# ScalarE takes over copies, the first convolution tap and the high parts in the first block

## The chip, the cores and the metric

The program runs on one core of a Trainium2 chip. The metric is the device time of one launch in microseconds (us). A core has TensorE (PE in the profile, its weight loads are PEld), VectorE (DVE), ScalarE (ACT), GpSimd (POOL) and SyncE (SP), which only issues transfers here. Each engine works through its own instructions in order, and they meet through semaphores.

## What is computed

Two transformer blocks stand behind each other. The change touches only the first mixer of the first one: a differential attention over 256 tokens with four heads, beside it a convolution and a gated linear recurrence in both directions, then one output projection over both.

```python
def even_mixer(h, ...):                      # shortened
    q, k, v, g, xr, gr = split(h @ w_in)     # 24 blocks of 128 channels, tokens along the free axis
    a = diff_attention(q, k, v, t5_table, lam, lam_init, subln_g)
    r = bidir_rglru(xr, conv_w, conv_b, w_a, b_a, w_x, b_x, lru_lambda)
    return concat(a * silu(g), r * silu(gr)) @ w_out

def diff_attention(q, k, v, ...):
    p = softmax(q @ k.T * scale + bias)      # two maps for each head
    out = (p[0] - lam * p[1]) @ v
    return rms_norm(out, subln_g) * (1.0 - lam_init)

def bidir_rglru(x, ...):
    xc = conv(x, conv_w, padding=(2, 1)) + conv_b        # four taps, per channel
    gate_a, gate_x = sigmoid(xc @ w_a + b_a), sigmoid(xc @ w_x + b_x)
    log_a = -8.0 * gate_a * softplus(-lam)
    u = sqrt(-expm1(2.0 * log_a)) * gate_x * xc
    return scan_forward(exp(log_a), u) + scan_backward(exp(log_a), u)
```

## The kernel before

Activations lie transposed: 128 channels on the partitions, tokens along the free axis. `ev` holds the 24 projected blocks, `xc` the four convolved ones, `OT` the four attention outputs, `gates`, `aT` and `tT` what the recurrence needs. Every matrix product is made to full precision out of three matmuls: a value x is split into a high part `Hh` (rounded to the fp32r type) and a low part `Hl` = x - Hh, and so is each weight tile (`Wh` by ScalarE at L526, `Wl` by VectorE at L811). `three` issues the three matmuls of one 128x128 block. The weight tiles come through `raw`, two slots of 1 MB.

The order of each engine is written out by hand and doesn't change at run time. A helper `link` makes VectorE wait for its own last instruction. The order around the change is this.

- **Convolution.** After the last tile of even_in, and after small work for lambda, VectorE makes for each of the four blocks one tensor_scalar (tap 2 and the bias, L1115) and three linked multiply-adds (L1116 to L1118, recorded at L798, as all its `scalar_tensor_tensor` are). Each block releases matmuls with the gate weights `lruw`; 16 products in all, whose tanh ScalarE makes into `gates` (L672). Meanwhile ScalarE has made the exponential for lambda (L658), copied the T5 row table and sent it out and in again by DMA (L662, L665), and copied the turned values `evtok` (L668).
- **Attention.** Four groups g of two query blocks make eight units u. TensorE: scores (u + 2), `mix` of the group before (in even units from 2 on), transposes of u. VectorE: `maxes` of u + 1, `normalise` of u, and in even units from 2 on `take` (L999), which waits for the mix and copies it from the PSUM tile `psN` to `OT`. ScalarE: `exps` of u + 1 (L610), two activations of the recurrence (`decay`, L677 and L678), `copies` of u (L625). The fourth mix and its take stand behind the loop.
- **Subnorm.** ScalarE squares `OT` (L681), makes the tanh of the gate, splits a weight tile and takes the square root that the recurrence needs (L687). TensorE sums the squares over channels, 16 matmul records on `psN`. VectorE multiplies the gates (two of 1024 columns, three of 2048, up to L1132), then computes the means (L1134). GpSimd raises them to -0.5, TensorE spreads the result.
- **Output projection.** VectorE scales `OT`, multiplies it by the gate (L1143), makes high and low part of each of its four blocks (L992, L993), then does the product with the square root, eight scans, a sum, and, after a tanh by ScalarE (L690), the last two products (L1157, L1158) and the parts of the other four blocks. `h_ready` counts the blocks with both parts. TensorE multiplies the first two tiles of even_out with blocks 0 to 3 (48 matmuls) when they come, and with 4 to 7 when these come.
- **SyncE.** In even_out it sends for each tile t: the weight tile t + 2, two gemv weights (`ada_w` or `mod_w`), each after a dot product of VectorE has freed a slot (L840), and from t = 1 on four loads of the neighbourhood bias `nab` (L411), the first after `h_ready` of all eight blocks.

## Time and profile before

| | |
|---|---|
| time, median of 3 runs | 2087.09 us (2086.03 to 2087.93) |
| profiled execution | 2086.57 us, span 2084.8 us |
| granted TensorE clock, mean | 0.961 |
| TensorE busy | 1910.5 us, 92% |
| VectorE busy | 1403.1 us, 67% |
| ScalarE busy | 683.8 us, 33% |
| GpSimd busy | 123.0 us, 6% |

The times of rows are microseconds from the start of the span. The profiled execution's time is 1.8 us longer than its span. Busy shares are means over stages with different limits. The stretch that the change touches lies between about 120 and 207 us, and what it releases reaches to about 250 us.

### The profile page before, as it was taken

The page shows a single profiled execution, that of the slowest core. Times are in us where ns is not written, and L with a number is a line of the kernel's source. Part 1 is how long each engine was busy: PE and PEld are TensorE (multiplying, and loading weights), DVE is VectorE, ACT ScalarE, POOL GpSimd, SP SyncE. Part 2 cuts the span into 40 slices and gives each one's busy share as a digit, 9 for nine tenths or more (in the row PEclk, how much of TensorE's full clock was granted, in tenths as well). Part 3 has the DMA queues.
Part 4 walks back from the last instruction along what each step waited for, and adds up shares of the span by engine and source line. Part 5 has one row for each costly group of instructions (what it writes and reads, how often), then busy time and mean ns, then how long its engine had stood idle before and what let it go on. Part 6 is the DMA issues. An engine that isn't in the chain of part 4 may idle for free.

```text
span 2084.8 us, 26715 instructions
## 1 busy us (share of the span) xinstructions
PE 1910.5 (92%) x10092; PEld 1624.6 (78%) x10092; DVE 1403.1 (67%) x2091; ACT 683.8 (33%) x910; POOL 123.0 (6%) x78
## 2 busy tenths in 40 slices
PE   2975799799999998997999999989999998889998
PEld 2954788678888887886888888878888887679998
DVE  7868899876666666668766666776665225856554
ACT  2443356332222223332322222132222123444432
POOL 2000200200000110002000001100000010010000
PEclk9976899899999999998999999999999999999999
DMA  9840955433334443434244334424433323223444
GB/s 377 309 176 26 247 193 198 156 120 141 133 148 148 154 172 121 151 131 159 113 151 149 133 140 168 167 110 151 151 138 115 101 93 120 91 81 141 164 162 158
DMA packets 75738, 315.79 MB, mean 151 GB/s; under 512 B 19060, under 2 KB 22904, under 8 KB 56344
## 3 DMA queue, kind: packets, MB, share of 16 engines
q1 hardware_dynamic: 75136, 314.15, 42.6%
q8 instruction: 37, 0.61, 0.1%
q10 hardware_dynamic: 536, 0.79, 0.1%
q14 instruction: 29, 0.24, 0.0%
HBM read 313.86 MB, written 1.06 MB: 151 GB/s over the span
## 4 chain that ended last, share of the span: by engine, by line
PE 74%; DVE 17%; ACT 3%; issue 2%; DMA 1%; SPq 1%; POOL 0%; DVEq 0%; ACTq 0%
PE acc L1296 72%; DVE Wl L811 4%; ACT Wh L526 2%; DVE tmp L798 2%; PE psN L1296 1%; DVE psGT L843 1%; DVE psGT L846 1%; DVE najunk L846 1%; DVE najunk L843 1%; DMA afirst<-in_ada_w 1%; DVE small L968 1%; DVE XT L798 1%; DVE psGT L840 1%; DVE tmp L986 1%; PE psN L1358 0%
## 5 line engine op out<-in xcount | busy, mean ns | idle before, releaser
L1296 PE MATMUL acc<-Hh,Wh 128*128 128x512 f32 (+1 forms) x2320 | 808.4, 348 | 50.1 <-DVE Hl L798 24.2
L1296 PE MATMUL acc<-Hl,Wh 128*128 128x512 f32 (+1 forms) x2320 | 800.3, 345 | 0.0
L1296 PE MATMUL acc<-Hh,Wl 128*128 128x512 f32 (+1 forms) x2320 | 799.6, 345 | 0.0
L811 DVE TENSOR_TENSOR Wl<-raw,Wh 128x2048 fp32r<-128x2048 f32 (+1 forms) x214 | 449.6, 2101 | 273.4 <-ACT Wh L526 273.3
L1296 PEld LDWEIGHTS acc<-Hh,Wh 128*128 128x128 f32 x2320 | 448.3, 193 | 113.7 <-issue 46.0
L526 ACT ACTIVATE Wh<-raw 128x2048 fp32r<-128x2048 f32 (+1 forms) x214 | 374.3, 1749 | 350.0 <-PE acc L1296 331.8
L1296 PEld LDWEIGHTS acc<-Hl,Wh 128*128 128x128 f32 x2320 | 448.6, 193 | 50.7 <-issue 0.7
L1296 PEld LDWEIGHTS acc<-Hh,Wl 128*128 128x128 f32 x2320 | 447.9, 193 | 50.4
L1296 PE MATMUL acc<-hidh,Wh 128*128 128x512 f32 (+1 forms) x704 | 258.6, 367 | 0.9 <-DVE Wl L811 0.9
L1296 PE MATMUL acc<-hidl,Wh 128*128 128x512 f32 (+1 forms) x704 | 258.3, 367 | 0.0
L1296 PE MATMUL acc<-hidh,Wl 128*128 128x512 f32 (+1 forms) x704 | 258.2, 367 | 0.0
L798 DVE SCALAR_TENSOR_TENSOR tmp<-tmp,acc 128x512 f32<-128x512 f32 (+1 forms) x176 | 109.4, 621 | 129.7 <-ACT tmp L593 120.0
L593 ACT ACTIVATE tmp<-acc 128x512 f32<-128x512 f32 (+1 forms) x88 | 47.9, 544 | 452.8 <-PE acc L1296 452.8
L843 DVE SCALAR_TENSOR_TENSOR psGT<-graw,cb 128x1024 f32<-128x1024 f32 x122 | 169.3, 1388 | 0.4
L459 POOL TENSOR_TENSOR tmp<-tmp 128x512 f32<-128x512 f32 (+1 forms) x44 | 90.1, 2049 | 1310.6 <-ACT tmp L557 1152.5
L846 DVE SCALAR_TENSOR_TENSOR psGT<-graw,cb 128x1024 f32<-128x1024 f32 x122 | 154.0, 1262 | 4.2
L1296 PEld LDWEIGHTS acc<-hidh,Wh 128*128 128x128 f32 x704 | 132.4, 188 | 25.1 <-DVE Wl L811 1.1
L1296 PEld LDWEIGHTS acc<-hidh,Wl 128*128 128x128 f32 x704 | 132.3, 188 | 23.9
L1296 PEld LDWEIGHTS acc<-hidl,Wh 128*128 128x128 f32 x704 | 132.4, 188 | 23.8
L935 DVE TENSOR_TENSOR hidl<-tmp,hidh 128x512 f32 (+3 forms) x88 | 55.1, 626 | 71.5 <-ACT hidh L596 71.5
L798 DVE SCALAR_TENSOR_TENSOR XT<-acc,mod,XT 128x256 f32 (+3 forms) x88 | 36.0, 455 | 88.5 <-PE acc L1296 88.5
L596 ACT ACTIVATE hidh<-tmp 128x512 f32 (+3 forms) x88 | 50.9, 578 | 134.1 <-DVE tmp L798 134.1
(222 smaller groups left out, 1189.9 us busy)
## 6 DMA issues: line engine op xcount, KB each, us to landing
raw<-in_ffn_up SPq DMA_DIRECT2D x88, 1024.0 KB, 4.8
graw<-in_mod_w SPq DMA_DIRECT2D x144, 512.0 KB, 5.5
raw<-in_ffn_down SPq DMA_DIRECT2D x64, 704.0 KB, 4.1
graw<-in_ada_w SPq DMA_DIRECT2D x32, 512.0 KB, 6.8
raw<-in_odd_in SPq DMA_DIRECT2D x16, 1024.0 KB, 5.0
raw<-in_even_in SPq DMA_DIRECT2D x12, 1024.0 KB, 7.2
raw<-in_conv_in SPq DMA_DIRECT2D x12, 1024.0 KB, 4.8
afirst<-in_ada_w SPq DMA_DIRECT2D x8, 1024.0 KB, 13.1
```

Of the source, the lines that this page charges most:

```text
L459: nc.gpsimd.tensor_tensor(tmp[:, 2, 0:n], tmp[:, 0 if k == 1 else 2, 0:n], tmp[:, k % 2, 0:n], ALU.add).then_inc(n_sum, 1)
L526: nc.scalar.activation(Wh[:, half, 0:f], raw[:, slot, 0:f], ACT.Copy).then_inc(hi_ready, 1)
L593: nc.scalar.activation(tmp[:, b, 0:s.tokens], acc[b][0][:, 0:s.tokens], ACT.Tanh, scale=0.5)\
L596: nc.scalar.activation(at3(hidh, t, s.tokens), tmp[:, 3, 0:s.tokens], ACT.Copy).then_inc(ffn_hi, 1)
L798: return nc.vector.scalar_tensor_tensor(out=out, in0=a, scalar=s, in1=b, op0=op0, op1=op1)
L811: nc.vector.tensor_tensor(Wl[:, half, 0:f], raw[:, slot, 0:f], Wh[:, half, 0:f].bitcast(f32), ALU.subtract)\
L840: nc.vector.scalar_tensor_tensor(out=psGT[:, :], in0=graw[:, slot, :], scalar=0.5, in1=cfirst[:, :], op0=ALU.mult, op1=ALU.mult, accum_out ...
L843: nc.vector.scalar_tensor_tensor(out=junk[:, :], in0=graw[:, slot, :], scalar=0.5, in1=cb[:, 0, :], op0=ALU.mult, op1=ALU.mult, accum_out= ...
L846: nc.vector.scalar_tensor_tensor(out=junk[:, :], in0=graw[:, slot, :], scalar=0.5, in1=cb[:, 1, :], op0=ALU.mult, op1=ALU.mult, accum_out= ...
L935: nc.vector.tensor_tensor(at3(hidl, t, c), tmp[:, 3, c], at3(hidh, t, c).bitcast(f32), ALU.subtract)\
L968: link(nc.vector.tensor_reduce(out=out, in_=L[:, u % 2, :, :], op=ALU.max, axis=AX.X))
L1296: return nc.tensor.matmul(out, lhsT, rhs, start=start, stop=stop)
```

## The change

In the first mixer some work passes from VectorE to ScalarE, and some work is cut or reordered.

- ScalarE writes tap 2 and the bias of all four convolution blocks, in one go behind the last projection copy and ahead of the exponential for lambda.
- ScalarE copies the four mixed outputs from `psN` to `OT` (`output`), in the loop behind `copies(u)`, the last one behind the loop. VectorE has no take in this attention any more.
- The high parts `Hh` of the eight blocks are written by ScalarE (`parts`): four behind the square root, four behind the tanh at L690. VectorE writes the low parts alone (`low_part`).
- The product of `OT` with its gate, one instruction of 1024 columns, becomes four of 256, each with a semaphore for ScalarE; the last product of the recurrence likewise.
- The low parts of blocks 0 to 3 come after the product with the square root, where both parts came before it.

```diff
+        lru_tap, ev_full, ev_hi = sem("lru_tap"), sem("ev_full"), sem("ev_hi")
...
+            def output(g):
+                act.wait_ge(diff.mixed, g + 1)
+                nc.scalar.activation(OT[:, g, :], psN[:, 0:LAT], ACT.Copy).then_inc(diff.taken, 1)
+
             def attention(a, beside=None):
                 exps(a, 0)
                 for u in range(a.units):
...
                     copies(a, u)
+                    if a is diff and u >= 2 and u % 2 == 0:
+                        output(u // 2 - 1)
+                if a is diff:
+                    output(a.groups - 1)
...
             project(S["even_in"], lambda m: at(ev, m), beside_even_in)
 
+            act.wait_ge(drained["act"], S["even_in"].drained1)
+            for c in range(4):
+                nc.scalar.activation(xc[:, c, :], ev[:, 16 + c, :], ACT.Identity, scale=V("conv_w", c * 4 + 2), bias=V("conv_b", c))\
+                    .then_inc(lru_tap, 1)
             act.wait_ge(lam_sum, 1)
...
             nc.scalar.activation(tT[:, :, :], tT[:, :, :], ACT.Sqrt).then_inc(lru_mult, 1)
+            def parts(c, x):
+                act.wait_ge(ev_full, c + 1)
+                nc.scalar.activation(Hh[:, c, 0:LAT], x, ACT.Copy).then_inc(ev_hi, 1)
+
+            for c in range(4):
+                parts(c, OT[:, c, :])
             act.wait_ge(lru_hs, 1)
 
             nc.scalar.activation(aT[:, 0:4, :], ev[:, 20:24, :], ACT.Tanh, scale=0.5).then_inc(ev_th, 1)
+            for c in range(4):
+                parts(4 + c, gates[:, 1, c, :])
...
-            def two_parts(k, value, width=LAT):
-
-                link(nc.vector.tensor_copy(Hh[:, k, 0:width], value))
-                nc.vector.tensor_tensor(Hl[:, k, 0:width], value, Hh[:, k, 0:width].bitcast(f32), ALU.subtract).then_inc(h_ready, 1)
+            def low_part(k, value):
+
+                dve.wait_ge(ev_hi, k + 1)
+                nc.vector.tensor_tensor(Hl[:, k, 0:LAT], value, Hh[:, k, 0:LAT].bitcast(f32), ALU.subtract).then_inc(h_ready, 1)
...
-                if a is diff:
-                    nc.vector.tensor_copy(OT[:, g, :], o).then_inc(a.taken, 1)
-                elif a is na:
+                if a is na:
...
-                    if u >= 2 and u % 2 == 0:
+                    if a is gqa and u >= 2 and u % 2 == 0:
                         take(a, u // 2 - 1)
-                take(a, a.groups - 1)
+                if a is gqa:
+                    take(a, a.groups - 1)
...
-                link(nc.vector.tensor_scalar(y, x, V("conv_w", c * 4 + 2), V("conv_b", c), ALU.mult, ALU.add))
+                dve.wait_ge(lru_tap, c + 1)
...
-            link(stt(OT[:, :, :], OT[:, :, :], 0.5, sga, ALU.mult, ALU.mult))
             for c in range(4):
-                two_parts(c, OT[:, c, :])
+                stt(OT[:, c, :], OT[:, c, :], 0.5, sga[:, c, :], ALU.mult, ALU.mult).then_inc(ev_full, 1)
             dve.wait_ge(lru_mult, 1)
             u_ = gates[:, 1, :, :]
             link(stt(u_, u_, 0.5, tT[:, :, :], ALU.mult, ALU.mult))
+            for c in range(4):
+                low_part(c, OT[:, c, :])
...
-            link(stt(gates[:, 1, 0:4, :], gates[:, 1, 0:4, :], 0.5, aT[:, 0:4, :], ALU.mult, ALU.mult))
             for c in range(4):
-                two_parts(4 + c, gates[:, 1, c, :])
+                stt(gates[:, 1, c, :], gates[:, 1, c, :], 0.5, aT[:, c, :], ALU.mult, ALU.mult).then_inc(ev_full, 1)
+            for c in range(4):
+                low_part(4 + c, gates[:, 1, c, :])
```

## Rows read from the trace of the kernel before

**Rows 1.** The page's chain that ended last, shares of the span by engine.

```profile
PE 74%; DVE 17%; ACT 3%; issue 2%; DMA 1%; SPq 1%; POOL 0%; DVEq 0%; ACTq 0%
```

**Rows 2.** Windows: stretch, length, busy time of each engine (instructions), clock, DMA share, GB/s.

```profile
core 0: us, PE busy (x) PEld busy (x) DVE busy (x) ACT busy (x) POOL busy (x), PEclk, DMA share, GB/s
142.02:171.63 29.61, 19.30 (x64) 9.93 (x64) 22.45 (x67) 19.07 (x56) 0.00 (x0) 0.67 0.00 0
...
188.85:206.57 17.72, 10.88 (x63) 10.68 (x64) 16.20 (x28) 1.06 (x1) 1.00 (x2) 0.70 0.00 1
206.57:235.86 29.29, 20.70 (x152) 20.00 (x151) 24.23 (x29) 10.05 (x12) 13.59 (x8) 0.91 1.13 240
```

**Rows 3.** Timeline, convolution: start, duration, engine, line, tiles, count, idle before and releaser.

```profile
123.89 0.20 ACT L658 ACTIVATE small<-small 128x2 f32<-128x2 f32 x1 [2.24 <-DVE small L1107]
...
124.70 0.41 DVE L1115 TENSOR_SCALAR xc<-ev_proj,vec 128x256 f32<-128x256 f32 x1
125.15 1.52 DVE L798 SCALAR_TENSOR_TENSOR xc<-ev_proj,vec,xc 128x254 f32<-128x254 f32 x3
126.59 0.40 DVE L1115 TENSOR_SCALAR xc<-ev_proj,vec 128x256 f32<-128x256 f32 x1
...
132.37 8.73 PE L1296 MATMUL acc<-xc,lruw 128*128 128x256 f32 x26 [0.66 <-DVE xc L798]
```

**Rows 4.** Groups by line and form, 124 to 206 us: count, busy us, mean ns.

```profile
L678 ACT ACTIVATE tT<-gates,small 128x256 f32<-128x256 f32 x8 | 4.7, 586 | 0.0
...
L993 DVE TENSOR_TENSOR Hl<-OT,Hh 128x256 fp32r<-128x256 f32 x4 | 1.7, 426 | 0.1
...
L992 DVE CAST Hh<-OT 128x256 fp32r<-128x256 f32 x4 | 1.2, 288 | 0.0
```

**Rows 5.** Timeline of the attention, VectorE and what it waits for.

```profile
154.08 0.42 DVE L999 COPY OT<-psN 128x256 f32<-128x256 f32 x1 [1.13 <-PE psN L1296]
...
154.43 0.74 DVE L798 SCALAR_TENSOR_TENSOR tmp<-acc,t5b 128x256 f32<-128x256 f32 x2
...
157.23 0.75 DVE L798 SCALAR_TENSOR_TENSOR tmp<-acc,t5b 128x256 f32<-128x256 f32 x2
...
160.54 0.42 DVE L999 COPY OT<-psN 128x256 f32<-128x256 f32 x1 [0.42 <-PE psN L1296]
...
167.39 0.37 ACT L625 ACTIVATE dP<-psGT 128x256 f32<-128x256 f32 x1
...
169.52 2.07 PE L1296 MATMUL psN<-dP,evtok 128*128 128x256 f32 x4 [0.47 <-ACT dP L625]
...
171.63 0.42 DVE L999 COPY OT<-psN 128x256 f32<-128x256 f32 x1 [3.33 <-PE psN L1296]
```

**Rows 6.** Timeline behind the attention, to the product of OT and gate.

```profile
171.97 2.47 DVE L798 SCALAR_TENSOR_TENSOR gates<-gates,xc 128x1024 f32<-128x1024 f32 x2
...
173.20 3.58 PE L1296 MATMUL psN<-ones,tmp 128*128 128x1 f32 x16 [1.61 <-ACT tmp L681]
...
180.28 0.16 DVE L1134 TENSOR_SCALAR means<-psN 128x8 f32<-128x8 f32 x1
...
186.70 1.22 DVE L798 SCALAR_TENSOR_TENSOR OT<-OT,tmp 128x1024 f32<-128x1024 f32 x1
```

**Rows 7.** Timeline of the output projection: ScalarE's tanh and the first dot product.

```profile
199.00 1.06 ACT L690 ACTIVATE aT<-ev_proj 128x1024 f32<-128x1024 f32 x1 [15.39 <-DVE gates L1155]
...
205.26 1.23 DVE L840 SCALAR_TENSOR_TENSOR psGT<-graw,cfirst 128x1024 f32<-128x1024 f32 x1
```

**Rows 8.** The chain in order of time: even_in's matmuls, even_out's with its fifth block.

```profile
99.99 15.22 PE acc L1296 x124
...
203.41 4.47 PE acc L1296 x24
```

**Rows 9.** Timeline of SyncE's queue, and the ScalarE split that waits for it.

```profile
218.07 9.40 SPq L411 DMA_DIRECT2D nab<-in_na_rpb  x4
227.52 1.45 SPq L373 DMA_DIRECT2D raw<-in_odd_in  x1
...
235.86 1.91 ACT L526 ACTIVATE Wh<-raw 128x2048 fp32r<-128x2048 f32 x1 [2.16 <-DMA raw<-in_odd_in]
```

## The prediction

> **What bounds the kernel now.** I read the page's chain first. It puts 74% of the span on TensorE and 17% on VectorE [rows 1], so a VectorE edit can pay only in a stretch in which TensorE waits. The windows show two such stretches in the first block: during the attention TensorE is busy for 19.30 of 29.61 us, and during the output projection the DMA engines are over full (share 1.13) [rows 2]. I then went through the timeline of each engine from 120 to 236 us, asking at each step what ended the wait. The reader is to see five stages, each started by the one before: the convolution on VectorE, which releases the gate matmuls [rows 3]; the attention, where VectorE's step and its copy of the mixed output alternate [rows 5]; a VectorE chain that ends in the means of the subnorm [rows 6]; the two halves of even_out, each released by a low part [rows 7, 8]; and a SyncE queue and transfers set off by VectorE's first dot product [rows 7, 9]. SyncE has nothing with a date of its own between 121 and 206 us: what it sends is released by VectorE or TensorE, and the DMA share is 0.00 from 188.85 to 206.57 [rows 2]. So time saved up to 206 us should stay saved.
>
> **Stage 1, the convolution.** Removed from VectorE: four tensor_scalars. A channel starts every 1.89 us (124.70 to 126.59), of which the tap with its link takes 0.45 (124.70 to 125.15) [rows 3]. A channel then takes 1.44, and the matmuls that the fourth releases at 132.37 start 4 x 0.45 sooner, at 130.57. **Gain 1.8.** TensorE has 26 matmul instructions in 8.73 us there without a break, so the gain passes through to the first score. ScalarE's new taps have per-partition scale and bias, as the decay at L678 has: 586 ns [rows 4], about 0.49 from one start to the next with the overlap, so 2.1 us in all. The next ScalarE work, the exponential of lambda, starts at 123.89 after 2.24 us of idleness [rows 3], so the last projection copy ends at 121.65, and the taps run from there to about 123.75. The cover is thus nearly used up: every tenth of a microsecond that the taps take beyond 2.2 delays that exponential, and with it the T5 transfers behind it and the whole VectorE chain. If the cover were gone the price would be all of 2.1, more than the gain; I charge nothing, and keep 0.3 for the range.
>
> **Stage 2, the attention.** Between takes, a VectorE step is 2.80 (154.43 to 157.23) [rows 5]. In a step with a take it also waits for the mix and copies: 1.13 + 0.42 the first time [rows 5], 0.42 + 0.42 the second [rows 5], and the third is a copy alone, less the 0.08 by which neighbours overlap: 1.5, 0.85 and 0.34. If VectorE stays last, the eighth normalise comes 2.7 earlier. ScalarE takes the copies over, at the length of its like copy dP from PSUM, 0.37 [rows 5]. They stand behind copies(u), which waits for a transpose that TensorE issues after the mix, so that output(g) finds its semaphore set; queued behind it are the exponentials of the next step. ScalarE is busy for 19.07 us in the eight steps [rows 2], 2.4 a step, and with the outputs 2.6, under 2.80. But around each mix the order copies, output, exponentials lies on the way to the next normalise, and there ScalarE gives back its 0.37 twice. At the end, copies(6) and mix(3) stand 2.13 apart now (167.39 to 169.52); then copy, output, two decays of 0.49 and copy fill 2.1 there, so this distance stays. **Gain 1.9**, with bounds 0 (ScalarE holds the old pace) and 2.7.
>
> **Stage 3, from the last mix to the means.** The last mix ends at 169.52 + 2.07 = 171.59. VectorE sat idle for it for 3.33 us, copied, and only then began the gate work that leads at 180.28 to the means [rows 5, 6]: 8.69 after the mix. That work (171.97 to 180.28, 8.31 long) needs nothing of the mix. Without the take it starts when the last normalise ends: 3.33 before the mix's copy, plus the 0.8 by which stage 2 brings VectorE further forward than the mix, so about 4.1 before the mix ends, and it is through 8.3 - 4.1 = 4.2 after it. Then another is late: the copy, the square and the 16 sums end at 173.20 + 3.58 = 176.78 [rows 6], 5.2 after the mix, and the copy is no longer on ScalarE than on VectorE. **Gain 8.69 - 5.2 = 3.5.** The square root on ScalarE comes after its split and a table load; its wait is for the same gate work, and its result is wanted only after the OT products, so it is covered by some 5 us. If stage 2 gains nothing, this stage still holds, because the TensorE sums set it.
>
> A rule of the Trainium skill bears on ScalarE's order here ("ScalarE: Activation LUTs", section "Table sets: the hidden batching unit"): copy and identity are in every table set, so the high parts right after the square root should load nothing. No run here shows a copy after a square root. By the rule nothing is added; if it failed, one more load would fall into ScalarE's idle time before the Tanh, and the sum would be the same.
>
> **Stage 4, OT to the second half of even_out.** One product of 1024 columns, 1.22 (186.70) [rows 6], becomes four of 256: a three-operand instruction of this size takes 0.48 and starts 0.40 after its neighbour where no link stands between (the three of a channel end at 125.15 + 1.52 = 126.67, the next starts at 126.59) [rows 3], so 4 x 0.40 instead of 1.24: +0.36. Casts go: a pair of cast and difference is 0.66, four pairs 2.65 (0.288 and 0.426 with their links) [rows 4]; four differences alone, 0.35 apart, are 1.4. Before the scans that is 2.65 - 1.4 - 0.36 = 0.9 saved. The gates product of 2048 columns now stands ahead of the low parts, and VectorE's high parts come from ScalarE, which has been idle for 15.39 us at its next instruction [rows 7] and has them ready meanwhile. The order delays the first half of even_out: with 7.2 gained up to here, the product of 186.70 starts at 179.5, the four parts of it end at 181.1, the gates product (2048 columns, as long as two of 1024 less one fixed part, 2.3) at 183.4, the first low part at 183.8. TensorE then needs 8.9 for 48 instructions at the pace of 24 in 4.47 [rows 8], until 192.7. The second half is released at 203.41 - 8.1 = 195.3, so the delay is covered by 2.6. Behind the Tanh, four products at 0.40 and a difference (2.03) stand for product, cast and difference (1.22 + 0.29 + 0.43), which cost 0.1 more with the split: nothing. **Gain 0.9.** The fourth difference, and with it the first dot (205.26) [rows 7], comes some 0.9 sooner still: the three pairs behind the first, 3 x 0.66, become 3 x 0.35.
>
> The fixed cost of small pieces is the rule that speaks against this change ("VectorE: DVE Perf Modes", section on the TRN2 errata: an SBUF-source instruction pays a fixed latency each, tiles of 512 or more amortise it). The trace agrees: 1024 columns take 1.22 and 256 take 0.48. By the page's formula (N+151)/0.96 a split would cost 4 x 0.424 - 1.224 = 0.47, an estimate; the total would be 0.1 less for each split.
>
> **Stage 5, SyncE and the transfers.** The two ada_w loads wait for the dots, and the bias loads stand behind them. Four bias loads take 9.40 us to issue, the second odd_in tile goes out at 227.52 and is used at 235.86 [rows 9], with the DMA engines full [rows 2]. So this stretch starts with the first dot, 8.1 + 0.9 = 9.0 earlier, but the dots of the second tile follow TensorE, 8.1 earlier, and SyncE waits for them once more. Result between 8.1 and 9.0; I take 8.8, as a full DMA queue bridges that wait.
>
> **The sum.** 1.8 + 1.9 + 3.5 + 0.9 = 8.1, and 0.7 of the 0.9: 8.8. The profiled execution took 2086.57 with a span of 2084.8; its span becomes 2076.0, its time 2077.8, and against the median of 2087.09, 0.5 above it, **2078.3**.
>
> **The rivals.** (a) ScalarE's order holds the attention at its old pace: 8.8 - 1.9 = 6.9, 2080.2. For it: ScalarE is busy for 19.07 of 29.61 us there and gets work inside a loop of waits. Against: 2.6 of work in 2.80. (b) The clock gives more: the granted clock is 0.67 in the attention [rows 2], so the engine changes between 1.2 and 2.4 GHz there; after its pause it runs even_out's second half at 24 instructions in 4.47 us, where 124 of even_in took 15.22 [rows 8], 2.95 for 24. With the pause cut to under 4 us it might start at the high level: up to 1.5 more, 10.3, 2076.8. (c) The gain is absorbed: the transfers of stage 5 stay where they are because the queue, not its start, sets their landing. For it: share 1.13, a landing of 8.3 us. Against: the DMA engines stand still before 206 us, so the stretch can start early. If the landing at 235.86 moved by half of the 9.0 only, less 0.5 for the wait on the second tile's dots, 4.0 would be left: 2083.1. (d) Slower, by the clock alone: granted clock falls in the stage after the change. A tile of odd_in has 48 instructions, 5.9 at the pace of even_in; at half the clock it costs up to 5.9 more. From two such tiles it eats the gain, and three make 17.7: 2096.0. For it: that stage begins after a pause and at the low level already. Against: nothing in the change makes later pauses longer. (e) The work moves to ScalarE without any wait of VectorE going: 1.8 + 0.9 + 0.9 alone, 3.6, which is less than can be told, 2083.5. Against it stands the idle time of 3.33 in rows 5.
>
> **How the numbers follow.** Forecast 0.55; (a) 0.17; (b) 0.15; (c) 0.05; (d) 0.03; (e) 0.05. Measurement tells 0.2%, 4.2 us, from no change. The forecast's own range is 8.1 to 9.6, less 0.3 for the taps: 2077.5 to 2079.3. With (a), its lower bound for stage 5 (6.2) and (b) with stage 2 at its upper bound (11.1), and up to 0.5 of scatter, the range is 2075.5 to 2081.5. Faster by over 0.2%: 0.55 + 0.17 + 0.15 = 0.87; within: 0.10; slower: 0.03.
>
> **What would show it.** The last convolution instruction near 130.5; ScalarE's taps over before 123.9; VectorE without idle time before an OT copy and the last mix ending near 167.9; the means near 173.1, released by the sums and no longer by VectorE; the first matmul of even_out near 183.8 and the fifth input block's near 195.3; the second odd_in tile used near 227. I am wrong if ScalarE's taps push the T5 chain, if exponentials start later in the loop, if the table is loaded more than three times on the path, or if odd_in's first matmul isn't some 8.8 earlier.

## The result and the profile after

The changed kernel takes a median of 2076.84 us (2075.76 to 2079.23, 5 runs) against 2087.49 for the kernel before on the same chip: the ratio is 0.9948, with a 95% interval from 0.9938 to 0.9959. By the ratio 10.9 us are gone, where 8.8 were forecast. The time lies inside the whole range, and is faster than the forecast's own range of 2077.5 to 2079.3. The profiled execution took 2075.76 with a span of 2073.9.

The page's part 4 of the changed kernel, the chain's shares:

```profile
PE 74%; DVE 18%; ACT 3%; issue 2%; DMA 1%; POOL 1%; SPq 0%; DVEq 0%; ACTq 0%
```

At 10 us in 2000 the shares tell nothing. The windows tell more. These are the attention, the stretch around even_out's two halves, and the stretch of the odd_in weights (share of the DMA engines and GB/s are the last two columns, the granted clock stands before them):

```profile
137.56:164.60 27.04, 16.63 (x64) 8.74 (x64) 24.74 (x67) 19.58 (x60) 0.00 (x0) 0.78 0.00 0
180.39:193.58 13.19, 9.53 (x58) 9.33 (x59) 11.97 (x23) 2.48 (x5) 1.00 (x2) 0.76 0.01 1
193.58:222.36 28.78, 20.60 (x146) 19.91 (x145) 24.23 (x29) 10.14 (x11) 13.30 (x8) 0.86 1.12 247
```

The attention shrank from 29.61 to 27.04 [rows 2]; ScalarE is busy for 19.58 in it, where it was for 19.07. The timeline of the changed kernel, convolution and attention (start, length, engine, line, operation, count, idle time before it and what ended it; TensorE, VectorE and ScalarE rows are picked out):

```profile
119.70 0.66 ACT L543 ACTIVATE ev_proj<-acc 128x256 f32<-128x256 f32 x2 [3.30 <-PE acc L1318]
120.39 2.07 ACT L668 ACTIVATE xc<-ev_proj,vec 128x256 f32<-128x256 f32 x4
122.60 0.20 ACT L671 ACTIVATE small<-small 128x2 f32<-128x2 f32 x1
123.41 5.82 DVE L819 SCALAR_TENSOR_TENSOR xc<-ev_proj,vec,xc 128x254 f32<-128x254 f32 x12
129.28 7.35 PE L1318 MATMUL acc<-xc,lruw 128*128 128x256 f32 x26 [0.21 <-DVE xc L819]
137.56 1.14 PE L1318 MATMUL acc<-ev_proj 64*128 64x256 f32 x8 [0.93 <-ACT gates L685]
...
148.41 0.75 DVE L819 SCALAR_TENSOR_TENSOR tmp<-acc,t5b 128x256 f32<-128x256 f32 x2
...
151.23 0.75 DVE L819 SCALAR_TENSOR_TENSOR tmp<-acc,t5b 128x256 f32<-128x256 f32 x2
...
154.04 0.75 DVE L819 SCALAR_TENSOR_TENSOR tmp<-acc,t5b 128x256 f32<-128x256 f32 x2
...
160.93 2.48 DVE L819 SCALAR_TENSOR_TENSOR gates<-gates,xc 128x1024 f32<-128x1024 f32 x2
162.49 2.07 PE L1318 MATMUL psN<-dP,evtok 128*128 128x256 f32 x4 [0.73 <-ACT dP L626]
164.60 0.38 ACT L631 ACTIVATE OT<-psN 128x256 f32<-128x256 f32 x1 [2.17 <-PE psN L1318]
166.12 3.58 PE L1318 MATMUL psN<-ones,tmp 128*128 128x1 f32 x16 [1.56 <-ACT tmp L694]
169.73 0.17 DVE L1154 TENSOR_SCALAR means<-psN 128x8 f32<-128x8 f32 x1 [0.41 <-PE psN L1318]
```

The reader is to see four things. The twelve convolution instructions stand in one row of 5.82, without the tap. ScalarE's taps are one row of 2.07 and the exponential follows them without a noted wait, 2.90 after the last projection copy as in before. VectorE's steps begin 2.82 and 2.81 apart (148.41, 151.23, 154.04) with and without a mix between them, where 154.08, 160.54 and 171.63 were copies with waits [rows 5]. And the gate work begins at 160.93, 3.63 before the last mix ends (162.49 + 2.07), so that the means are released by TensorE's sums and no longer by VectorE [rows 6].

The output projection of the changed kernel, the same view:

```profile
176.16 1.43 DVE L819 SCALAR_TENSOR_TENSOR OT<-OT,tmp 128x256 f32<-128x256 f32 x4
176.61 1.43 ACT L703 ACTIVATE Hh<-OT 128x256 fp32r<-128x256 f32 x4 [4.57 <-DVE OT L819]
177.50 2.28 DVE L819 SCALAR_TENSOR_TENSOR gates<-gates,tT 128x2048 f32<-128x2048 f32 x1
178.06 1.28 ACT L709 ACT_TABLE_LOAD   x1
179.82 1.43 DVE L1014 TENSOR_TENSOR Hl<-OT,Hh 128x256 fp32r<-128x256 f32 x4
180.39 0.55 PE L1318 MATMUL acc<-Hh,Wh 128*128 128x256 f32 x1 [5.84 <-DVE Hl L1014]
191.40 0.58 PE L1318 MATMUL acc<-Hh,Wh 128*128 128x256 f32 x1 [3.66 <-DVE Hl L1014]
192.27 1.23 DVE L861 SCALAR_TENSOR_TENSOR psGT<-graw,cfirst 128x1024 f32<-128x1024 f32 x1
222.36 1.89 ACT L527 ACTIVATE Wh<-raw 128x2048 fp32r<-128x2048 f32 x1
```

Four products of 256 columns take 1.43, and so do the four low parts. The second odd_in tile is used at 222.36 without a wait, where at 235.86 the transfer was waited for [rows 9].

**Where the time went.** I compare by the distances between events, since the last even_in copy came at 120.99 in the profiled execution of before, at 119.70 here, and anywhere from 119.35 to 120.99 in the fourteen traces of this study: nothing changed ahead of it, so that is the execution's scatter. All in us, worked out from the starts in the traces; "before, again" is a second execution of the same kernel, taken with the last group of experiments:

```
                                              forecast gain  before  before, again   after
last even_in copy -> first score                   1.8        21.03      20.70       17.86
first score -> last mix                            1.9        27.50      28.02       24.93
last mix -> means                                  3.5        10.76      10.76        7.24
means -> fifth block's first matmul                0.9        23.13      23.13       21.67
sum                                                8.1        82.42      82.61       71.70
means -> first dot                                 1.8        24.98      24.98       22.54
fifth block -> first tile of even_out complete     -           4.56       5.58        5.58
that tile -> norm means of odd_in                  -          28.88      28.61       28.62
norm means of odd_in -> end of the span            -        1848.0     1849.0      1848.3
last even_in copy -> end of the span               8.8      1963.8     1965.8      1954.2
```

Up to the fifth block 10.7 are gained against the first execution of before, 10.9 against the second. Behind it the changed kernel is like the second execution of before to 0.01 up to the norm means. The first one differs in three places, none of them the change's doing: it is 1.02 faster to the complete tile, 0.26 slower to the norm means, and from there to the first scaled block 3.18 pass, where both others have 4.38 (e5 and e6 take this up). What follows scatters by up to 0.9 more. So by the last row 9.6 are gained against one execution and 11.6 against the other.

### The profile page after: what moved, and what is told of

It is laid out like the page before. It is cut to its first block, busy times and chain, and to the rows that moved or that the text cites. A ratio compares the mean times of both kernels' runs of the same rounds, so it can differ in the third digit from the quotient of the medians.

```text
span 2073.9 us, 26722 instructions
## 1 busy us (share of the span) xinstructions
PE 1906.5 (92%) x10092; PEld 1621.9 (78%) x10092; DVE 1397.0 (67%) x2081; ACT 689.9 (33%) x926; POOL 128.0 (6%) x78
## 4 chain that ended last, share of the span: by engine, by line
PE 74%; DVE 18%; ACT 3%; issue 2%; DMA 1%; POOL 1%; SPq 0%; DVEq 0%; ACTq 0%
PE acc L1318 72%; DVE Wl L832 4%; ACT Wh L527 2%; DVE tmp L819 2%; PE psN L1318 1%; DVE psGT L861 1%; DVE psGT L867 1%; DVE psGT L864 1%; DVE najunk L867 1%; DVE najunk L864 1%; DVE small L989 1%; DVE XT L819 1%; DMA afirst<-in_ada_w 1%; PE psN L1380 1%; DVE tmp L1007 1%
```

## The experiments

Eight kernels change the changed kernel (e), three the kernel before (f2 to f4), and f1 is the kernel before again. Times are medians; the ratio is to the kernel before on the same chip. The e kernels from e1 to e4 were run beside 2088.06 for before, e5 to e8 beside 2087.71, the f kernels beside 2087.77. Two medians of different groups are thus from different chips, and each ratio of e1 to e8 is known only to 0.001 to 0.0017 either way, 2 to 3.5 us. The changed kernel's interval is 0.9938 to 0.9959. Of the e kernels only e3 lies clear of it by its time; for the others the differences of medians are not told from scatter, and the distances in the traces carry the reading.

### e1: the taps back on VectorE

```diff
-            act.wait_ge(drained["act"], S["even_in"].drained1)
-            for c in range(4):
-                nc.scalar.activation(xc[:, c, :], ev[:, 16 + c, :], ACT.Identity, scale=V("conv_w", c * 4 + 2), bias=V("conv_b", c))\
-                    .then_inc(lru_tap, 1)
...
-                dve.wait_ge(lru_tap, c + 1)
+                link(nc.vector.tensor_scalar(y, x, V("conv_w", c * 4 + 2), V("conv_b", c), ALU.mult, ALU.add))
```

> The changed kernel with the first tap of the convolution back on VectorE, all else as changed. Measured from the start of ScalarE's last copy of even_in, the changed kernel releases the fourth channel's gate matmuls after 9.6 us and starts the first score after 17.9 us; the kernel before needed 11.4 and 21.0. Theory: the tap is worth 4 x 0.45 = 1.8 us at the fourth channel (11.4 again) and the other 1.4 us at the first score is the TensorE clock that rises earlier when the gate matmuls stand closer together, so the first score goes back to about 21.0 and the time is 1.8 to 3.2 above the changed kernel. Rival: the 1.4 us is chance of the clock from run to run; then the first score comes 1.8 later only (19.7).

**Measured:** 2079.77, ratio 0.9961 (0.9947 to 0.9975), 2.9 above the changed kernel. Copy to first score is 21.10, so 3.24 come back there and not 1.8; the loop behind it takes 25.08. The 26 gate matmuls take 8.79, where they took 7.35.

### e2: three of the four outputs back on VectorE

```diff
-                    if a is diff and u >= 2 and u % 2 == 0:
-                        output(u // 2 - 1)
...
-                if a is na:
+                if a is diff:
+                    nc.vector.tensor_copy(OT[:, g, :], o).then_inc(a.taken, 1)
+                elif a is na:
...
-                    if a is gqa and u >= 2 and u % 2 == 0:
+                    if u >= 2 and u % 2 == 0:
                         take(a, u // 2 - 1)
```

> The changed kernel with VectorE taking the first three mixed outputs again inside the loop, and ScalarE only the last. Theory: the last mix starts some 2.6 us later relative to the first score (24.9 us in the changed kernel, 27.5 before), and VectorE's gate work behind the loop, being later by 2.7, ends about when the sums of TensorE do; means and all that follows 2.6 to 3 later. Rival: the pace of the loop was set by TensorE's clock (granted 0.78 against 0.67), so the last mix comes less than 1 us later.

**Measured:** 2080.72, ratio 0.9961 (0.9947 to 0.9975), 3.9 above the changed kernel. First score to last mix is 28.47, 3.54 longer; every other distance is the changed kernel's. The three copies of e2 on VectorE in its timeline:

```profile
150.00 0.42 DVE L1018 COPY OT<-psN 128x256 f32<-128x256 f32 x1 [1.11 <-PE psN L1318]
...
156.99 0.42 DVE L1018 COPY OT<-psN 128x256 f32<-128x256 f32 x1 [0.94 <-PE psN L1318]
...
163.55 0.42 DVE L1018 COPY OT<-psN 128x256 f32<-128x256 f32 x1 [0.51 <-PE psN L1318]
```

The waits are 1.11, 0.94 and 0.51, where [rows 5] have 1.13 and 0.42, and the third copy there came without one. A copy behind a wait costs the wait and its full 0.42, so these terms make 3.82. VectorE is that much later: the reciprocal of the last unit, with which its normalise begins, starts 25.94 after the first score, 22.13 in the changed kernel. The last mix is only 3.54 later, since with e2 ScalarE's third output copy is gone as well. It had pushed back by 0.27 the last of ScalarE's copies of the turned weights to `dP`, for which the last mix waits.

### e3: the last output back on VectorE

```diff
-                if a is diff:
-                    output(a.groups - 1)
...
-                if a is gqa:
-                    take(a, a.groups - 1)
+                take(a, a.groups - 1)
```

> The changed kernel with only the last mixed output taken by VectorE again, which then waits for the last mix before its gate work. Theory: the last mix stays where it is, the means come 8.7 us after its end instead of 5.2: 3.5 us, and the time is some 3.5 above the changed kernel. Rival: the gain behind the loop came out of the earlier loop; then the time is less than 1 us above.

**Measured:** 2081.47, ratio 0.9972 (0.9963 to 0.9982), 4.6 above by the medians and 4.6 by the spans (2078.5 and 2073.9). Last mix to means is 10.76, as before the change, which is 3.52 of it, and the loop keeps its 24.93. The rest stands behind the norm means (1849.8 to the end of the span against 1848.3), where e3 changes nothing and the two executions of before differ by 1.1. VectorE's timeline in e3:

```profile
164.17 0.42 DVE L1018 COPY OT<-psN 128x256 f32<-128x256 f32 x1 [3.59 <-PE psN L1317]
164.51 2.47 DVE L817 SCALAR_TENSOR_TENSOR gates<-gates,xc 128x1024 f32<-128x1024 f32 x2
...
172.82 0.16 DVE L1153 TENSOR_SCALAR means<-psN 128x8 f32<-128x8 f32 x1
```

VectorE stands for 3.59 with the gate work queued behind the copy, and is again the last at the means. The place of one instruction of 0.42 is worth 3.52.

### e4: product, casts and differences as before

```diff
-            for c in range(4):
-                parts(c, OT[:, c, :])
...
-            for c in range(4):
-                parts(4 + c, gates[:, 1, c, :])
...
+            link(stt(OT[:, :, :], OT[:, :, :], 0.5, sga, ALU.mult, ALU.mult))
             for c in range(4):
-                stt(OT[:, c, :], OT[:, c, :], 0.5, sga[:, c, :], ALU.mult, ALU.mult).then_inc(ev_full, 1)
+                two_parts(c, OT[:, c, :])
...
-                low_part(c, OT[:, c, :])
...
+            link(stt(gates[:, 1, 0:4, :], gates[:, 1, 0:4, :], 0.5, aT[:, 0:4, :], ALU.mult, ALU.mult))
             for c in range(4):
-                stt(gates[:, 1, c, :], gates[:, 1, c, :], 0.5, aT[:, c, :], ALU.mult, ALU.mult).then_inc(ev_full, 1)
-            for c in range(4):
-                low_part(4 + c, gates[:, 1, c, :])
+                two_parts(4 + c, gates[:, 1, c, :])
```

> The changed kernel with the output projection as before: one product of 1024 columns, high and low part both by VectorE, ahead of the product with the square root. Theory: between the OT product and the fifth block's first matmul 1.5 us come back (16.7 in place of 15.2), the first dot is 2.4 later, but the second half of even_out may run at the higher TensorE clock again for part of its way (24 instructions in 4.5 us instead of 5.5), so the first matmul of odd_in is only 0.5 to 1.5 later, the time 2077.3 to 2078.5. Rival: the clock has nothing to do with it; then the time is 1.5 to 2.4 above the changed kernel.

**Measured:** 2078.93, ratio 0.9962 (0.9948 to 0.9976), 2.1 above the changed kernel. Means to fifth block is 23.13 (1.46 back) and means to first dot 24.98 (2.44 back). The split of the first half in e4's timeline:

```profile
177.34 1.22 DVE L811 SCALAR_TENSOR_TENSOR OT<-OT,tmp 128x1024 f32<-128x1024 f32 x1
178.60 0.29 DVE L1005 CAST Hh<-OT 128x256 fp32r<-128x256 f32 x1
178.93 0.43 DVE L1006 TENSOR_TENSOR Hl<-OT,Hh 128x256 fp32r<-128x256 f32 x1
179.27 0.28 DVE L1005 CAST Hh<-OT 128x256 fp32r<-128x256 f32 x1
...
181.26 2.28 DVE L811 SCALAR_TENSOR_TENSOR gates<-gates,tT 128x2048 f32<-128x2048 f32 x1
```

From the product's start to the gates product 3.92 pass here. In the changed kernel 1.34 pass, and the low parts, which follow later, put 1.35 between the gates product and the first scan (179.82 to 181.17): 1.23 less in all up to the scans. The other 0.24 is behind the Tanh, where from the product's start to the fifth block 2.06 pass in before (201.35 to 203.41) and 1.82 in the changed kernel (189.58 to 191.40).

### e5 and e6: the split of an odd_in tile out of the norm's chain

By the trace of the changed kernel the stretch behind the first half ends in this chain (VectorE, then GpSimd, in the timeline of the changed kernel):

```profile
225.60 0.16 DVE L897 TENSOR_SCALAR means<-psN 128x4 f32<-128x4 f32 x1 [4.33 <-PE psN L1380]
225.68 2.28 DVE L832 TENSOR_TENSOR Wl<-raw,Wh 128x2048 fp32r<-128x2048 f32 x1
225.84 2.68 POOL L452 TENSOR_TENSOR rctx<-means,expo 128x2 f32<-128x2 f32 x1 [6.70 <-DVE means L897]
```

GpSimd's power on two columns takes 2.68 while VectorE's split reads two arrays in SBUF; in the trace of before the same power took 0.71, and the split began 0.79 after the end of the means instead of at once. e5 moves the split ahead of the wait for the sums, e6 behind the loop that scales the blocks.

```diff
 # e5
+                if name == "odd_in":
+                    split(S[name].n0 + 1, early=True)
                 dve.wait_ge(n_ss, i + 1)
...
-                split(S[name].n0 + 1, early=True)
+                if name != "odd_in":
+                    split(S[name].n0 + 1, early=True)
 # e6
-                split(S[name].n0 + 1, early=True)
+                if name != "odd_in":
+                    split(S[name].n0 + 1, early=True)
...
                     ins.then_inc(h_ready, 1)
+                if name == "odd_in":
+                    split(S[name].n0 + 1, early=True)
```

> The changed kernel with VectorE's split of odd_in's second weight tile moved ahead of its wait for the sums (in the norm ahead of odd_in only). In the changed kernel GpSimd's first power takes 2.68 us beside that split, against 0.71 in the kernel before, where the tile came late and the split started after the powers. Theory: the two engines slow each other; with the split out of the way the power takes 0.7 again, the split fills VectorE's wait of 4.3 us, the means come about 1 us later and the first scaled block some 1.2 us earlier. Rival: the power is long for another reason (code of that instruction cold, a busy memory); then it stays at 2.7 and the scaled block comes 1 us later.

> The changed kernel with the same split moved behind the norm's eight blocks. Theory: the power takes 0.7, the first scaled block comes 2.0 us earlier, and odd_in's first tile ends 2.0 earlier; but the second tile's split is then done some 2.3 us after the norm, later than TensorE wants it, and VectorE's masks and dots are pushed behind it, so 1 us or more is given back on the second tile. Rival (the power is long for another reason): 2.7 stays, and nothing comes earlier.

**Measured:** e5 2076.06, ratio 0.9947 (0.993 to 0.9964); e6 2076.96, ratio 0.9949 (0.9933 to 0.9966). Neither can be told from the changed kernel. The timeline of e5:

```profile
225.41 2.29 DVE L832 TENSOR_TENSOR Wl<-raw,Wh 128x2048 fp32r<-128x2048 f32 x1 [3.80 <-ACT Wh L527]
227.62 0.15 DVE L899 TENSOR_SCALAR means<-psN 128x4 f32<-128x4 f32 x1
227.85 0.71 POOL L452 TENSOR_TENSOR rctx<-means,expo 128x2 f32<-128x2 f32 x1 [8.37 <-DVE means L899]
```

and of e6:

```profile
225.97 0.71 POOL L452 TENSOR_TENSOR rctx<-means,expo 128x2 f32<-128x2 f32 x1 [6.70 <-DVE means L897]
...
235.73 2.29 DVE L832 TENSOR_TENSOR Wl<-raw,Wh 128x2048 fp32r<-128x2048 f32 x1
237.94 1.95 DVE L1195 TENSOR_TENSOR nab<-nab,namask 128x768 f32<-128x768 f32 x2
```

The power takes 0.71 in both, so the split beside it was what stretched it. In e5 the split had to wait 3.80 for ScalarE's high part of the tile, and the means, behind the split, come 1.68 later; the first scaled block follows them after 2.39 instead of 4.38, 1.99 sooner. In e6 the first scaled block stands 2.40 behind the means. Of these 2 us nothing is left later on: from the norm means to the first square of the next norm pass 149.64 in the changed kernel (4.38 + 9.04 + 136.22) and 150.01 in e6 (2.40 + 9.25 + 138.36). VectorE's queue has hardly a gap from here on, and the split that e6 puts behind the blocks lies in it at 235.73, ahead of the mask products, which therefore start at 237.94 where the changed kernel had them at 237.58. That this queue is where the 2 us go is argued from these rows; no run shows it.

### e7: the low parts before the product with the square root

```diff
             for c in range(4):
                 stt(OT[:, c, :], ...).then_inc(ev_full, 1)
+            for c in range(4):
+                low_part(c, OT[:, c, :])
             dve.wait_ge(lru_mult, 1)
...
-            for c in range(4):
-                low_part(c, OT[:, c, :])
```

> The changed kernel with the low parts of blocks 0 to 3 ahead of the product with the square root, as the parts stood before. Theory: the first half of even_out starts 2.2 us earlier, but the second half is released by the same VectorE chain, so the fifth block, first dot and time stay within 0.3 us of the changed kernel, apart from a wait of some tenths for ScalarE's high part. Rival: the shorter pause of TensorE in the changed kernel matters for its clock, and the longer one (5.9 us in place of 3.7) makes the second half slower.

**Measured:** 2076.39, ratio 0.9947 (0.9931 to 0.9964), equal to the changed kernel. TensorE in e7's timeline:

```profile
178.01 0.55 PE L1318 MATMUL acc<-Hh,Wh 128*128 128x256 f32 x1 [3.52 <-DVE Hl L1014]
...
191.33 0.58 PE L1318 MATMUL acc<-Hh,Wh 128*128 128x256 f32 x1 [4.97 <-DVE Hl L1014]
```

The first half starts 13.32 ahead of the second instead of 11.01, and the pause before the second becomes 4.97 instead of 3.66; means to fifth block stays at 21.66. The delay that the change puts on the first half costs nothing. The second half is as slow as in the changed kernel, 5.58 to its completion.

### e8: two more copies at each of three outputs

```diff
             def output(g):
                 act.wait_ge(diff.mixed, g + 1)
+                if g < 3:
+                    nc.scalar.activation(Hh[:, 2 * g + 0, LAT:TOK], psN[:, 0:LAT], ACT.Copy)
+                    nc.scalar.activation(Hh[:, 2 * g + 1, LAT:TOK], psN[:, 0:LAT], ACT.Copy)
                 nc.scalar.activation(OT[:, g, :], psN[:, 0:LAT], ACT.Copy).then_inc(diff.taken, 1)
```

The extra copies go to a part of `Hh` that nothing reads then.

> The changed kernel with two more copies of the mixed output by ScalarE (into an unused part of Hh) ahead of each of the first three copies: 3 x 2 x 0.3 us more work for ScalarE inside the attention loop. Theory (ScalarE has slack at 2.6 of 2.8 us a step, but lies on the way around each mix): most of the 1.8 us shows at the last mix, because copies, output and exponentials follow one another: 1.0 to 1.8 later. Rival: VectorE sets the loop and ScalarE's extra work is hidden: below 0.6 later.

**Measured:** 2078.80, ratio 0.9957 (0.994 to 0.9973), 2.0 above the changed kernel. First score to last mix is 26.86, 1.93 longer, where six copies, each 0.27 after its neighbour, are 1.6. VectorE hardly feels them: its steps stay at 2.81 or 2.82 but for one of 3.03, and its gate work begins only 0.64 later after the first score. What has grown is the chain of ScalarE and TensorE around the mixes: from the dP copy of unit 2 to that of unit 4, and on to that of unit 6, 6.01 and 6.02 pass (150.45, 156.46, 162.48), where two steps of VectorE are 5.62. So two more copies at a mix are not covered. How much of the 1.93 is theirs stays open, since the second and the third mix take 2.08 each here and 1.13 in the changed kernel, at a lower clock.

### f1 to f4: the kernel before again, and with one part of the change each

f1 is the kernel before unchanged (one run, so no ratio). f2 has ScalarE's taps alone, f3 the four outputs alone, f4 the split product with ScalarE's high parts and the new order alone; the edits are those parts of the diff above.

> The kernel before once more, for a second trace of it: what of the differences is chance. In its first trace the gate matmuls took 8.73 us, the second half's first 24 matmuls 4.56, GpSimd's first power 0.71, and the second odd_in tile came late. Theory: the waits of VectorE's chain are the same to 0.1 us (first score to last mix 27.5, mix to means 10.8, means to fifth block 23.1); what TensorE's clock and the DMA engines set may differ by up to 1 us, the power by 2.

> The kernel before with only the first tap moved to ScalarE. Theory: the fourth channel's matmuls are released 9.6 us after the last projection copy instead of 11.4, TensorE's clock rises earlier within them, and the first score comes 3.2 us earlier (17.9), the time 2.5 to 3.4 below the kernel before. Rival (clock by chance): 1.8 earlier.

> The kernel before with only the four output copies moved to ScalarE. Theory: first score to last mix 24.9 instead of 27.5, mix to means 7.2 instead of 10.8, so the means 6.1 earlier relative to the first score, and the time 5 to 6.5 below the kernel before. Rival: the loop's gain needs the other edits' clock; then the loop gives under 1.5 and the total 4 to 5.

> The kernel before with only the output projection changed (products in four pieces, high parts by ScalarE, low parts later). Theory: means to fifth block 21.7 instead of 23.1, the first dot 2.4 earlier, but what follows is timed by the fifth block and VectorE, so the time is 1 to 1.7 below the kernel before, not 2.4. Rival: the earlier dot and its transfers count in full; then 2.4 or more.

**Measured,** with the four distances of each:

```
                    median   ratio (95%)               copy->score  score->mix  mix->means  means->fifth
f1 before, again    2088.07  (one run)                    20.70       28.02       10.76       23.13
f2 taps alone       2085.17  0.9987 (0.9978 to 0.9997)    18.11       28.54       10.76       23.13
f3 outputs alone    2081.85  0.9971 (0.9961 to 0.9982)    20.69       25.08        7.24       23.14
f4 parts alone      2085.89  0.9990 (0.9981 to 1.0)       20.64       28.04       10.76       21.66
changed             2076.84  0.9948 (0.9938 to 0.9959)    17.86       24.93        7.24       21.67
```

Each part moves its own distance and leaves the others but for up to half a microsecond. By the ratios the parts make 0.0013 + 0.0029 + 0.0010 = 0.0052, as much as 1 - 0.9948, but each is known only to about 0.001, and that of f4 isn't told from nothing. By the medians 2.6 come from the taps, 5.9 from the outputs, 1.9 from the parts. The distances are sharper: added up to the fifth block's first matmul, f2 is 2.07 below f1, f3 6.46 and f4 1.51, together 10.04, and the changed kernel is 10.91 below. The taps alone gain 2.59 at the first score and give 0.52 back in the loop, because the second mixed output is waited for longer there (1.00 in f2, 0.51 in f1); without takes in the loop nothing is given back. The rows of the gate matmuls, in f1 and in f2:

```profile
131.83 8.40 PE L1296 MATMUL acc<-xc,lruw 128*128 128x256 f32 x26 [0.66 <-DVE xc L798]
```

```profile
130.05 7.60 PE L1301 MATMUL acc<-xc,lruw 128*128 128x256 f32 x26 [0.21 <-DVE xc L803]
```

The same 26 instructions take 8.40 without the taps moved and 7.60 with them, and between two channels TensorE stands for 0.66 without and 0.21 with them; they take 7.27 to 7.92 in the nine traces where the taps are on ScalarE, and 8.34 to 8.79 in the five where they are not.

## Why the prediction was right in direction and short by two microseconds

**Stage 1 (1.8 forecast, 2.6 to 3.2 measured).** The release of the matmuls moved as worked out: from the last projection copy to the end of the fourth channel pass 11.38 in before and 9.58 in the changed kernel, 1.80 less. The step that failed is "so the gain passes through to the first score": it took the 26 matmuls as 8.73 either way. They run at a granted clock of 0.67 in before, 0.69 in f1, 0.77 in f2 and 0.79 in the changed kernel, so partly at 1.2 and partly at 2.4 GHz, and ahead of them TensorE now stands for 0.21 between two channels instead of 0.66. That is worth another 0.8 (f1 against f2) to 1.4. That it goes with the taps is shown, in all fourteen traces; that the shorter pauses are what does it is my reading, and no run sets the pauses by themselves. Nor is the extra gain the same everywhere: in e4 and e6 the matmuls take 7.92 and 7.88 and the first score comes 18.43 and 18.39 after the copy, but there the last mix takes 1.13 instead of 2.07, and from the copy to the means 50.11 and 50.06 pass, against 50.03 in the changed kernel. The cover on ScalarE was as thin as said: 2.07 of taps from 120.39 to 122.46, the exponential at 122.60.

**Stage 2 (1.9 forecast, 2.6 to 3.5 measured).** The mechanism is right, and two sizes were off. "There ScalarE gives back its 0.37 twice" was too much: VectorE's steps stay at 2.81 or 2.82 across each mix, and only the last dP copy is pushed back, once, by the 0.27 that the output copy ahead of it takes up. With this the sum closes. The reciprocal of the last unit starts 24.97 after the first score in before, 25.49 in f1 and 22.13 in the changed kernel, 2.84 and 3.36 sooner (2.7 forecast); the last mix comes 2.57 and 3.09 sooner. And the waits were read from one execution that happened to have the shortest ones: 1.13, 0.42 and none [rows 5], where f1 shows 1.13, 0.51 and 0.49, and e2 1.11, 0.94 and 0.51. What is left without takes is the same to 0.2 in every kernel but e8 (24.91 to 25.08), so the change removes the waits whatever they were. The upper bound of 2.7 was thus a bound of one execution and not of the kernel. The thought behind the give-back has its truth in e8: with three copies at a mix the chain through ScalarE is the longer one. Between one copy and three its slack ends; where was not tried.

**Stage 3 (3.5 forecast, 3.5 measured).** 10.76 became 7.24. The forecast of what is late next held: the copy on ScalarE, the square and the 16 sums end at 169.70, 5.14 after the mix (5.2 forecast), and VectorE waits 0.41 for them. e3 and f3 show it by both sides. The margin was thinner than forecast: VectorE began its gate work 3.63 and not 4.1 before the end of the mix, since the mix had come nearly as far forward as VectorE, and was through 4.8 and not 4.2 after it. In e4 and e6, where the last mix takes 1.13, VectorE is the last at the means again, 6.76 after the start of the mix.

**Stage 4 (0.9 forecast, 1.5 measured).** Two terms were mis-sized. The split product was priced at 4 x 0.40 from the convolution's instructions [rows 3], which multiply by a per-partition scalar from SBUF and take 0.48. The product multiplies by the constant 0.5 and takes 0.42, as the differences do: 

```profile
L819 DVE SCALAR_TENSOR_TENSOR OT<-OT,tmp 128x256 f32<-128x256 f32 x4 | 1.4, 419 | 0.0
L1014 DVE TENSOR_TENSOR Hl<-OT,Hh 128x256 fp32r<-128x256 f32 x4 | 1.4, 420 | 0.0
```

These are groups by form of the changed kernel (count, busy time, mean ns of one, idle time before). With the overlap of 0.08 the next instruction starts 1.34 after the first of the four, where it started 1.25 after the one product in before (186.70 to 187.95): the split costs 0.09 there and not 0.36. The four pairs were rightly counted as 2.65 (2.66 in e4, 178.60 to 181.26), and the four differences put 1.35 ahead of the scans, 1.4 forecast. So before the scans 2.66 - 1.35 - 0.09 = 1.22 are saved where 0.9 was forecast, which is what the traces show (186.70 to 192.93 in before, 176.16 to 181.17 in the changed kernel). Behind the Tanh, which I called nothing, it is 0.24: the same cheaper product, and a first difference that follows without a link. That the order of the first half's low parts is covered is shown by e7, and that the split and ScalarE's high parts together pay by the distances of f4 and e4; no run has the split alone. By the rule on small pieces cited in the prediction ("VectorE: DVE Perf Modes" of the Trainium skill, section on the TRN2 errata) the split would cost 0.47, an estimate. The trace agrees with its length of one piece (0.424 by the formula, 0.419 in the row) and not with the sum, as neighbours overlap: four pieces are 0.21 longer than one product (1.43 and 1.22), and what follows starts 0.09 later. On the table sets the rule of the Trainium skill ("ScalarE: Activation LUTs", section "Table sets: the hidden batching unit") agrees: the copies at 176.61 follow the square root with no load, and the load stands at 178.06, behind them.

**Stage 5 (0.7 of 0.9 forecast, nothing measured).** This is the step that was wrong, in its mechanism. I let SyncE's issues and full DMA engines carry the stretch, started by the first dot. The first dot did come 2.44 sooner relative to the means, 0.98 more than the fifth block, but nothing followed it: the norm means of odd_in stand 28.60 to 28.62 behind the completion of the first tile in eleven of the fourteen traces, with 28.88 in before and 28.92 in f2, where VectorE's third split waits 0.17 and 0.22 for a tile that landed late, and 30.30 in e5, whose edit moves the means. What carries the stretch is VectorE: a split and two dots for each of three tiles, from 198.93 to 221.27 without a noted wait, then the square and TensorE's sums. SyncE's load lies beside it. In before the second odd_in tile was waited for [rows 9], and VectorE stood 0.79 for its split; in the changed kernel it is there in time. But so it is in f1, the same kernel as before, so that this isn't the change's doing. f4 and e4 price it: the parts are worth 1.9 to 2.1 with 1.46 at the fifth block, so the extra lead of the dot brings at most half a microsecond, which is within what medians tell here.

**The rivals.** (a) fell: the loop is faster by more than forecast. (b) named the time (2076.8) and not the reason. It put the gain into the second half of even_out; its 24 matmuls took longer in the chain of the changed kernel (start, length, what) than the 4.47 of [rows 8]:

```profile
191.40 5.50 PE acc L1318 x24
```

That is a loss of 1.0 against this execution: in the changed kernel the granted clock is 0.50 from 191.40 to the completion, the low level throughout, behind a pause of 3.66. Over all traces the step from the fifth block to the complete tile is 4.56 to 4.73 in before, e1, e6 and f4, 5.00 and 5.09 in e8 and f2, and 5.50 to 5.59 in the others, f1 among them, so it doesn't go with the edit. Among the eight traces whose halves start 11.0 apart it does go with the pause, and in (b)'s direction: 4.71 to 5.00 behind pauses of 2.92 to 3.20, 5.58 behind 3.66 to 3.72. But there a short pause also means a first half of 7.8 to 8.1 instead of about 7.3, so the two aren't told apart, and in the other six it doesn't hold (4.56 behind 6.84, 5.58 behind 7.23). The clock did give more, but in the gate matmuls. (c) and (e) are refuted by the time, and (d) did not occur: granted clock over the span is 0.965, where it was 0.961.

**The sum.** The time came inside the range with two errors of opposite sign: stages 1 to 4 brought 10.7 to 10.9 where 8.1 was forecast, and stage 5 nothing where 0.7 was.

**Open.** When TensorE's clock rises in even_out's second half, and what decides it, was not settled; it moves a trace by 1 us. Nor is it settled why the waits of the takes were 0.9 to 1.0 at the second mix in f2 and e2 and 0.4 to 0.5 in before, f1 and f4; both f2 and e2 have the taps on ScalarE, so a different phase of the clock behind the gate matmuls would fit, but no run isolates it. No version of this study is told apart as faster than the changed kernel (e5 with 2076.06 and e7 with 2076.39 are within its scatter).

## What to carry to other kernels

A short copy that an in-order engine must wait for costs the wait, not its own 0.42 us: look for independent work queued behind such an instruction, and give the copy to an engine that must follow the producer anyway (here 5.9 us by the medians, of 10.4 for the three parts, came from four copies). Before sizing such waits, look at more than one execution, since one may show a wait of 0 where the next shows 0.5. And ask of a lead that an edit creates which engine's queue is continuous behind it: the DMA engines were full and SyncE busy, and still it was VectorE's own row of splits and dots that set the date.

## What the runs showed of the hardware

**A tiny GpSimd instruction beside a VectorE one with two SBUF inputs.** The power on 128x2 takes 0.71 alone (e5, e6) and 2.68 when VectorE's 2.28 split starts 0.16 before it (the changed kernel; f1 shows it in the kernel before too, where the first trace had missed the overlap by chance and so was 1.2 sooner at the first scaled block). The rows of f1:

```profile
237.34 2.28 DVE L811 TENSOR_TENSOR Wl<-raw,Wh 128x2048 fp32r<-128x2048 f32 x1
237.51 2.69 POOL L451 TENSOR_TENSOR rctx<-means,expo 128x2 f32<-128x2 f32 x1 [6.70 <-DVE means L876]
```

The power ends about 0.6 after the split does, its own 0.71 less a little, as if it had begun only then. This is what the Trainium skill says ("SBUF — State Buffer", section "SBUF: two separate sides"): a VectorE operation with two SBUF inputs and a GpSimd operation that reads SBUF share a port pair, and whichever starts first holds it as an exclusive lock for its whole length. The reverse is in the same traces: VectorE's dot of 1.23 takes 2.33 at 201.14 in the changed kernel, where GpSimd's addition of 512 columns (2.29, from 200.08) is under way. In the row of splits and dots that carries stage 5, five of six dots take 2.03 to 2.33, 4.9 us more than five of 1.23, with an addition under way at each. What moving the additions would bring was not tried.

**The level of TensorE's clock can change by an edit to another engine.** The same 26 gate matmuls took 7.27 to 7.92 us at a granted clock of 0.74 to 0.80 in the nine traces where VectorE released a channel every 1.43, and 8.34 to 8.79 at 0.66 to 0.70 in the five where it released one every 1.89.

**The kind of the scalar shows in VectorE's time.** Three operands and 256 columns take 0.42 with a constant and 0.48 with a per-partition scalar from SBUF.
